# A hybrid decoder block on one core: one product for the bias rows, a prologue in order of arrival, and the next quarter's transposes moved among the last output tiles

## The reference

```
x   (2048, 1024)
h = rms_norm(x, g) ; z = h @ w_in        # 2304 columns: qa ka va | qr kr vr gr | up
A: 6 query heads, 2 key heads, window 128, blocks of 128, sinks,
   scores = q k^T / 8 + rel_bias[t5_bucket(dist)] , masked to 0 <= dist < 128
B: 6 retention heads in chunks of 128 with a carried 64x64 state, rotary, per-head norm, swish gate
C: trailing means over 2/4/8/16 positions, a 64x64 map per group
x = x + concat(A, B, C) @ w_out
x = x + relu(rms_norm(x) @ w_up)^2 @ w_down
return rms_norm(x, g_final)
```

## Time and profile before

| | |
|---|---|
| time, median of 3 runs (lowest to highest) | 2121.13 us (2120.67 to 2122.97) |
| the profiled execution: its own time, its span | 2121.23 us, 2119.4 us |
| PE busy | 2053.6 us (97%) |
| DVE, ACT, POOL busy | 1318.5, 918.5, 440.6 us |
| mixer: first product of quarters 0, 1, 2, 3 | 23.34, 232.48, 444.99, 653.40 us |
| end of the last output tile of the mixer | 858.57 us |

### The profile page before, as it was taken

One profiled execution on the slowest core, in us unless ns is written; L12 is line 12 of the kernel. 1 busy time (PEld: TensorE's weight loads), 2 busy tenths in 40 slices (PEclk: granted clock), 3 DMA queues, 4 the chain that ended last, 5 costly groups with the idle time before them and its releaser, 6 DMA issues.

```text
span 2119.4 us, 28140 instructions
## 1 busy us (share of the span) xinstructions
PE 2053.6 (97%) x10220; PEld 1728.1 (82%) x10220; DVE 1318.5 (62%) x1844; ACT 918.5 (43%) x1557; POOL 440.6 (21%) x363
## 2 busy tenths in 40 slices
PE   8998999999989998999999999999999999999998
PEld 6987798779877987788888888888788888888886
DVE  3346434643464447777777867777667757766666
ACT  4433443344334432654554654444433334433333
POOL 6256525652565355000000000000000000000001
PEclk9999999999999999999999999999999999999999
DMA  7132412241225122357776656677975667856562
GB/s 265 61 100 75 170 53 97 75 170 52 98 75 179 65 75 100 99 147 182 171 168 148 151 137 153 160 193 190 308 287 214 247 246 290 352 199 254 223 271 87
DMA packets 101956, 349.13 MB, mean 165 GB/s; under 512 B 10395, under 2 KB 12220, under 8 KB 84412
## 3 DMA queue, kind: packets, MB, share of 16 engines
q1 hardware_dynamic: 97212, 330.54, 48.5%
q10 hardware_dynamic: 4608, 16.78, 2.1%
HBM read 270.61 MB, written 76.68 MB: 164 GB/s over the span
## 4 chain that ended last, share of the span: by engine, by line
PE 85%; DVE 6%; issue 3%; POOL 3%; DMA 2%; ACT 1%; SPq 0%; ACTq 0%; DVEq 0%; POOLq 0%
PE bank L1977 27%; PE bank L1979 26%; PE bank L1978 26%; PE bank L2091 1%; PE bank L2120 1%; DMA d_raw<-in_wdn 1%; DVE pt L1449 1%; PE bank L2105 1%; PE bank L2208 1%; POOL r L809 1%; PE bank L2168 1%; DVE xq L1507 1%; DMA wraw<-in_wup 1%; POOL R L800 1%; DVE zt L1411 0%
## 5 line engine op out<-in xcount | busy, mean ns | idle before, releaser
L1977 PE MATMUL bank<-h_hi,w_lo 128*128 128x512 f32 x912 | 356.3, 391 | 1.8 <-ACT tA L1085 1.8
L1978 PE MATMUL bank<-h_lo,w_hi 128*128 128x512 f32 x912 | 355.1, 389 | 0.0
L1979 PE MATMUL bank<-h_hi,w_hi 128*128 128x512 f32 x912 | 355.1, 389 | 0.0
L1977 PE MATMUL bank<-d_hi,u_lo 128*128 128x512 f32 x896 | 349.0, 390 | 4.0 <-DVE d_lo L1849 4.0
L1979 PE MATMUL bank<-d_hi,u_hi 128*128 128x512 f32 x896 | 348.6, 389 | 0.0
L1978 PE MATMUL bank<-d_lo,u_hi 128*128 128x512 f32 x896 | 348.6, 389 | 0.0
L753 POOL TENSOR_TENSOR ring_lo<-stage,ring_hi 128x1024 fp32r<-128x1024 f32 x104 | 246.1, 2396 | 282.9 <-ACT ring_hi L905 282.8
L1226 ACT ACTIVATE u_hi<-u_raw 128x1024 fp32r<-128x1024 f32 x112 | 118.5, 1058 | 333.9 <-PE bank L1979 318.8
L883 POOL TENSOR_TENSOR var<-ssum,epsc 128x1 f32<-128x1 f32 x16 | 3.9, 241 | 1237.3 <-ACT sqj L1241 1237.3
L1849 DVE TENSOR_TENSOR u_lo<-u_raw,u_hi 128x1024 fp32r<-128x1024 f32 x112 | 137.0, 1223 | 179.6 <-ACT u_hi L1226 179.6
L1977 PE MATMUL bank<-ring_hi,hT_lo 128*128 128x384 f32 (+1 forms) x672 | 244.8, 364 | 0.2
(11 more groups left out here) (194 smaller groups left out, 3365.6 us busy)
## 6 DMA issues: line engine op xcount, KB each, us to landing
u_raw<-u_dram SPq DMA_DIRECT2D x56, 1024.0 KB, 4.8
d_raw<-in_wdn SPq DMA_DIRECT2D x56, 1024.0 KB, 6.9
stage<-in_wmix SPq DMA_DIRECT2D x108, 512.0 KB, 3.4
u_dram<-ur SPq DMA_DIRECT2D x32, 1280.0 KB, 9.4
wraw<-in_wup SPq DMA_DIRECT2D x128, 256.0 KB, 3.3
e_raw<-in_wdn SPq DMA_DIRECT2D x24, 1024.0 KB, 8.9
xn<-in_x SPq DMA_DIRECT2D x16, 512.0 KB, 4.8
xq<-in_x ACTq DMA_DIRECT2D x16, 512.0 KB, 6.0
```

Source lines behind the costliest of these rows:

```text
L1977: pe.matmul(dst, al, bh, start=(first and k == 0), stop=False, skip_group_check=chain)
L1978: pe.matmul(dst, ah, bl, start=False, stop=False, skip_group_check=chain)
L1979: last = pe.matmul(dst, ah, bh, start=False, stop=(final and k == n - 1), skip_group_check=chain)
```

## The change

What it does, by place:

- Bias: the 33x6 table is the stationary operand of one matmul whose result is 6 partitions x 384. DVE copies these 6 rows once. The store to DRAM reads each of the 6 rows 128 times.
- Prologue: SP issues the gain, the identity and `xn` 1 ahead of the bias tables; `mhalf` and `epsc` are set by POOL. ACT, DVE and PE take the blocks in order of arrival. The first two units are split by ACT and POOL before the loop.
- `norm_bank` uses (S0, S1) and (T1, OB) in turn. `norm_transposes`, `x_hi` and `x_lo` leave the head of a quarter; for the next quarter they stand among output tiles 12 to 15, in the last quarter not at all. `x_hi(b)` there waits for output tile 9 + 2b, since it writes over what the tile reads.
- `y_transposes` stand later: 0 behind tile 5, 1 behind `ret_outs(2)`, 2 behind tile 11, 3 behind tile 13. On DVE `yR_low` 0 and 1 stand later, `norm_ahead` earlier.
- Unit 28 (unit 1 of the next quarter) is split at the quarter's end; the loads of `xq` on ACT's queue move from the quarter's head to its first group tiles.

The diff, cut (counters renamed to `2 * NB * ahead + 2 * b + j`, and the last quarter's order on ACT, are left out):

```diff
         def norm_bank(b, j):
-            return ((T0, T1), (S0, S1), (dense[1], dense[2]), (OB, T0))[b][j]
+            return ((S0, S1), (T1, OB))[b % 2][j]
...
             sp.dma_start(xn[:, 0, :], x[0:P, :]).then_inc(x_full[0].sem, 16)
+            sp.dma_start(grow[:, :], gmix.to_broadcast([P, D])).then_inc(s_gain, 16)
+            sp.dma_start(ident[:, :], cview("ident")).then_inc(s_ident, 16)
+            sp.dma_start(xn[:, 1, :], x[P:2 * P, :]).then_inc(x_full[1].sem, 16)
             sp.dma_start(oneh, onehot).then_inc(s_rel, 16)
             sp.wait_ge(s_init, 1)
             sp.dma_start(relb[0:NBUCKET, :], rel_bias).then_inc(s_rel, 16)
-            sp.dma_start(mhalf[:, :], cview("mhalf")).then_inc(s_ident, 16)
-            sp.dma_start(epsc[:, :], cview("eps")).then_inc(s_ident, 16)
-            sp.dma_start(ident[:, :], cview("ident")).then_inc(s_ident, 16)
-            sp.dma_start(grow[:, :], gmix.to_broadcast([P, D])).then_inc(s_gain, 16)
-            for b in range(1, NB):
+            for b in range(2, NB):
...
-            sp.wait_ge(s_brow, NQH)
-            sp.dma_start(rows_dram.rearrange("h (p m) -> p h m", m=384), rrow).then_inc(s_rowst, 16)
+            sp.wait_ge(s_brow, 1)
+            sp.dma_start(rows_dram.rearrange("h (p m) -> h p m", m=384),
+                         rrow.rearrange("h (a m) -> h a m", a=1).to_broadcast([NQH, P, 384])).then_inc(s_rowst, 16)
...
     (POOL, end of a quarter)
-                for b in range(1, NB):
-                    inv_rms2(q, b)
+                inv_rms2(q, 1)
+                inv_rms2(q, 2)
+                if not last:
+                    split_lo(q, NU + 1)
+                inv_rms2(q, 3)
...
     (ACT)
             def mixer_act(q, last):
-                for b in range(NB):
-                    x_hi(q, b)
-                split_hi(q, 1)
                 split_hi(q, 2)
-                for b in range(NB):
-                    load_x(q, b)
...
                 square_x2(q, 0, last)
-                yR_high(q, 3)
-                if not last:
-                    square_x(q, NB + 3)
-                square_x2(q, 1, last)
...
+                else:
+                    square_x(q, NB + 3)
+                    square_x2(q, 1, last)
+                    x_hi(q, 0, True)
+                    yR_high(q, 3)
+                    x_hi(q, 1, True)
+                    x_hi(q, 2, True)
+                    square_x2(q, 2, last)
+                    x_hi(q, 3, True)
+                    split_hi(q, NU + 1)
+                    square_x2(q, 3, last)
...
     (DVE)
                 yP_low(q, 0)
-                yR_low(q, 0)
                 rot_a(q, 2)
                 rot_add(q, 2)
                 evac_x2(q, 5)
+                yR_low(q, 0)
...
                 decay_scores(q, 3)
+                evac_x2(q, 10)
+                norm_ahead(q, 0, last)
+                norm_ahead(q, 1, last)
+                evac_x2(q, 11)
                 yR_low(q, 2)
...
+                    x_lo(q, 0, True)
+                    evac_x2(q, 13)
+                    yR_low(q, 3)
+                    x_lo(q, 1, True)
                     norm_ahead(q, 3, last)
+                    x_lo(q, 2, True)
+                    evac_x2(q, 14)
+                    evac_x2(q, 15)
+                    x_lo(q, 3, True)
...
     (DVE, prologue)
-            for h in range(NQH):
-                if h == 4:
-                    x_norm(0, 0)
-                dve.wait_ge(s_browmm, h + 1)
-                dve.tensor_copy(rrow[:, h, :], bank[h][:, 0:384]).then_inc(s_brow, 1)
+            x_norm(0, 0)
+            x_norm(0, 1)
+            x_lo(0, 0, False)
+            x_norm(0, 2)
+            dve.wait_ge(s_browmm, 1)
+            dve.tensor_copy(rrow, bank[0][0:NQH, 0:384]).then_inc(s_brow, 1)
+            x_norm(0, 3)
...
     (PE)
                 pool_mix(q, 0)
+                out_tile(q, 5)
                 y_transposes(q, 0)
-                out_tile(q, 5)
...
                 ret_scores(q, 2)
-                y_transposes(q, 1)
                 out_tile_8_rest(q)
                 ret_outs(q, 2)
+                y_transposes(q, 1)
+                out_tile(q, 9)
                 qk_transposes(q, 3)
-                out_tile(q, 9)
+                out_tile(q, 10)
                 ret_scores(q, 3)
+                out_tile(q, 11)
                 y_transposes(q, 2)
-                out_tile(q, 10)
                 ret_outs(q, 3)
-                out_tile(q, 11)
                 out_tile(q, 12)
-                y_transposes(q, 3)
                 if closing:
                     h_transposes(0, 0)
+                else:
+                    norm_transposes(q, 0, True)
                 out_tile(q, 13)
+                y_transposes(q, 3)
                 if closing:
                     h_transposes(0, 1)
                     h_transposes(0, 2)
+                else:
+                    norm_transposes(q, 1, True)
+                    norm_transposes(q, 2, True)
                 out_tile(q, 14)
...
                 out_tile(q, 15)
+                if not closing:
+                    norm_transposes(q, 3, True)
...
     (PE, prologue)
+            norm_transposes(0, 0, False)
+            norm_transposes(0, 1, False)
+            pe.wait_ge(s_rel, 32)
+            pe.wait_ge(s_init, 1)
+            pe.matmul(bank[0][0:NQH, 0:384], relb, oneh, start=True, stop=True).then_inc(s_browmm, 1)
+            norm_transposes(0, 2, False)
+            norm_transposes(0, 3, False)
+            pe.wait_ge(s_brow, 1)
```

More of the change, by code:

```diff
@@ L745, in _ @@
             pool.wait_ge(s_pm, 6)
-            pool.wait_ge(s_ident, 48)
+            pool.wait_ge(s_half, 2)
             def split_lo(q, u):
@@ L831, in mixer_pool @@
             def mixer_pool(q, last):
-                for u in range(1, 6):
+                for u in range(2, 6):
                     split_lo(q, u)
@@ L938, in square_x2, with x_hi @@
                                accum_out=ssum2[:, bass.ds(q * NB + b, 1)]).then_inc(sq2_done.sem, 1)
-            def x_hi(q, b):
+            def x_hi(q, b, ahead):
+                if ahead:
+                    act.wait_ge(tile_done.sem, tile_done.now(q, T_OA + 9 + 2 * b))
                 for j in range(2):
[L942 to L945, removed]
+                    act.wait_ge(xtr_done.sem, xtr_done.now(q, 2 * NB * ahead + 2 * b + j))
                     act.activation(hT_hi[:, 4 * j:4 * j + 4, b * P:(b + 1) * P],
@@ L1156, in mixer_act @@
                             split_hi(q, 12 + 3 * (i // 2) + u)
+                    if i == 0:
+                        for b in range(NB):
+                            load_x(q, b)
                 yA_high(q, 3)
@@ L1198, in mixer_act @@
                     h_high(0, 1)
-                square_x2(q, 3, last)
-            for b in range(NB):
-                square_x(0, b)
+                    square_x2(q, 3, last)
+                else:
+                    square_x(q, NB + 3)
+                    square_x2(q, 1, last)
+                    x_hi(q, 0, True)
+                    yR_high(q, 3)
+                    x_hi(q, 1, True)
+                    x_hi(q, 2, True)
+                    square_x2(q, 2, last)
+                    x_hi(q, 3, True)
+                    split_hi(q, NU + 1)
+                    square_x2(q, 3, last)
+            square_x(0, 0)
+            square_x(0, 1)
+            x_hi(0, 0, False)
+            square_x(0, 2)
+            square_x(0, 3)
+            x_hi(0, 1, False)
             split_hi(0, 0)
+            x_hi(0, 2, False)
+            x_hi(0, 3, False)
+            split_hi(0, 1)
             with act.Fori(0, NQ - 1) as q:
@@ L1563, in mixer_dve @@
             def mixer_dve(q, last):
-                for b in range(NB):
-                    x_lo(q, b)
                 dve.wait_ge(o_done.sem, o_done.before(q, 3))
@@ L1965, in _ @@
                 pe.sem_inc(e.sem, e.primed)
-            pe.wait_ge(s_rel, 32)
-            pe.wait_ge(s_relw, 1)
-            for h in range(NQH):
-                pe.matmul(bank[h][:, 0:384], relw[:, h, :], oneh, start=True, stop=True).then_inc(s_browmm, 1)
-            pe.wait_ge(s_ident, 48)
-            pe.wait_ge(s_brow, NQH)
+            pe.wait_ge(s_ident, 16)
             def three(dst, pairs, first=True, final=True, chain=False):
```

82 lines of the change are left out of this document (34 added, 48 removed).

## The result

Four runs each: before 2121.78 us, after **2142.73 us** (2138.42 to 2146.93). The ratio is 1.0099, 95% interval 1.0087 to 1.0111. The forecast was 2108.0, range 2099.5 to 2115.5, so the sign was wrong as well.

What follows compares the result with a forecast made beforehand. PE was taken as the bound, with about 11 us open per mixer quarter, partly at low clock. Terms -6.1 - 5.45 - 1.8 + 1.1 - 1 = -13.25 on 2121.23 gave 2108.0 us, range 2099.5 to 2115.5.

Steps and rivals of the forecast that it cites:

- part 4: Prologue: first product at 19.5 to 20.7, tile 3 at 39 instead of 40.3; -1 us, between -4 and +2.
- rival (c): Prologue: slow bias store holds the weights, clock still low; quarter 0 gains nothing or loses 2; 2111 us, 17%.
- Part 1: First three quarters up to the end of tile 12: moving the y transposes is worth 0 in all.
- Rival (b): Mixer: low clock takes more behind the longer wait for the pool remainder; +9 us, 2117, chance 10%.
- Part 2: Changes of quarter, tile 12 to the next first product: gains of 6.1, 5.45 and 1.8 us.
- Part 3: Last quarter: tile 12 later and the second h_transposes waiting for yR_low(3); +1.1 us in sum.
- (a): Among the output tiles: the waits on y really go, 33.7 us gained in all; 2087.5 us, chance 3%.
- (d): Quarter's end: ACT's queue is held by a late load ahead of work tile 14 needs; 2126 us, 3%.
- (e): Waits added at the change of quarter (1.1 each) don't come, or the prologue keeps 3 to 4: 2103 us, 15%.

Runs made afterwards that it cites:

- e2: The changed kernel with the bias store reading six source partitions four apart (0, 4, 8, 12, 16, 20) instead of 0 to 5: 2113.99 us.
- e1: The changed kernel with the bias store reading 96 partitions, 8 copies each, instead of 6 with 128 copies each: 2113.94 us.
- e5: e1 with the moves of y transposes (blocks 0 to 2), block 3's qk transposes and yR_low 0 to 2 undone: 2101.42 us.
- e9: e1 with DVE's second pool remainder ahead of ret_y(1), and decay_scores(1) through yR_low(0) ahead of evac_x2(4) and (5): 2092.39 us.

## Why the prediction was wrong

**The step that failed: part 4, the bound of the store.** "From 6 partitions it may be as fast (3.5) or, were only 6 of the 16 DMA engines used, 9.4": the store took 34.3. The upper bound let each of the six engines go at the pace of the earlier trace rows, where all 128 partitions were read (and that row counts other loads too: 2.33 MB moved from 14.4 to 21.9 us, of which the store is 1.18). e2 shows that bound to be about right for six partitions that lie apart. It left out that neighbouring source partitions share a lower rate, 25 to 27 GB/s for a group, and no row of before reads so few. The value taken, "With 7.6 us, the row nearest", came from a row unlike it in the one thing that the change altered, the number of source partitions. The mechanism was right and stands as rival (c), with the threshold of 16 us from the row copy to SP's release. From the row copy, just before 16.09, to SP's release (50.41 + 2.72 = 53.1) it is 37 us, 21 over, and tile 3 came 23.0 us later than before. That e1 against after gives 28.8 is because tile 3 could have come 3 us sooner than before, and because PE then ran 5.3 us at half speed (63.31 to 68.6). Rival (c) ended at 2111 because it used the same bound of 9.4; e2, with the store back in 9.8 us, is as fast as e1, so at that price next to nothing was to be lost (0.65 us at tile 3).

**Part 4 otherwise.** First product at 19.71, forecast 19.5 to 20.7. The slow start at the first product took about 0.6 us, not 2: in e1 the products follow each other every 0.21 us from 19.88 to 21.32 and every 0.12 after. The prediction read such a pace as low clock. The profile's rows don't bear this out: they give the granted clock as 1.00 there, as they do in the earlier trace rows, so what makes PE slow in the prologue stays open. Tile 3 in e1 waited for nothing.

**Part 1, "0 in all".** The waits were walked rightly one by one: y(0) gave next to nothing, since PE then waits for the decayed scores before `ret_outs(1)`, 0.63 us in after and 0.98 in e1 (forecast 0.2 at most gained), the wait for y(1) went over to the pool remainder at 3.95 us (forecast 4.0), y(2)'s went. The `qk` transposes came 1.1 us later in e1, counted from `ret_outs(0)`, and 0.8 in after, not 0.6. What failed is the sum: waits were added as if each cost only its length. In e1 PE ran at the low level for 17 us more than in e5, 10 of them behind the `qk` wait of 2.0 and the remainder's 3.95 and 7 behind the wait for `hx`. Rival (b) named the clock, with 10% and 9 us; the size is near (8.5), the place only in part. Against e5 the moves cost 12.5 us, waits and clock together.

**Part 2.** Tile 12 to the first product: 16.5 us at the first change, forecast 15.5, before 19.8. y(3) waited 1.1 instead of 0.6, tile 14 not at all, and 0.86 us pass before the first product for which the trace names no releaser; that wait was not in the sum. It stands at both changes that are jumps back of the loop (0.86 and 0.63 us) and not at the third, which is none. In e1 the second of them, 0.95 us, is put down to DVE's last remainder for the next quarter. The clock stayed at full as forecast. At the third change 15.4 us, forecast 15.45.

**Part 3.** From the end of tile 12 to the first product of the second half e1 takes 22.4 us, before 21.5: +0.9, forecast +1.1. Over all, the last piece of the table is 4 us longer in after and e1 than in before; in e5 it is 0.1 longer. So e5 puts the rest of that down to part 1 as well, 3.4 us of it through the low spell behind `hx` whose cause is open.

**The other rivals.** (a) and (d) did not come; no load of `xn` held ACT.

**The whole.** With the store repaired and part 1 undone (e5) the rest of the change gives 20 us. The forecast for that rest was 13.3. The prologue gave 3.4 instead of 1, the changes of quarter 1 us less each, and the low clock shrank by 20.5 us, worth 10, where 3.6 had been counted: 13.3 + 2.4 - 2 + 6.6 is 20.3. That the sum fits is partly luck: the terms overlap, as part of the low clock lies within the changes of quarter, and no run parts them. So e1, only 6 us above the forecast, hides a part 1 that costs 12.5 and a rest that gives 7 more than forecast.

**Two sums of the range.** (e) with both its parts is 3 x 1.1 = 3.3 us of waits and 2 to 3 of prologue, so 2101.7 and not 2099.5, and half of (b)'s 9 us is 2112.5 and not 2115.5. The measured time lies far outside of either range.

## What to carry to other kernels

When an edit shrinks the number of partitions that a DMA reads, price the transfer by the bytes that each group of neighbouring partitions has to give, not by the rate of a wide transfer. Spread the source: in e1 that cost a broadcast copy of 0.2 us. Ask what the queue that waits for the landing has behind it. And when waits are moved, add the half-speed time behind each to its length: a wait that grows from 1 to 2 us may cost more than the wait.

## What the runs showed of the hardware that was not expected

Six source partitions side by side: 34.3 us for 1.18 MB, 50 and then 25 GB/s. Six that are four apart: 9.8 us, 151 GB/s. Ninety-six: 6.3 us. One at a time: 27 GB/s with the DMA engines 85% busy, 42.9 us. A busy DMA engine was thus no sign that bytes were moving fast.

The granted clock answers to small changes of order: 0.54 against 0.95 over the same 8 us, after waits of 3.95 and 3.29 us, with spells of 9 and of 3 us. Between before and e9 the low time falls from 37.5 to 3.4 us. Why a spell comes behind one wait and not behind another of like length (before has one of 3.2 to 3.3 us in each quarter, with 3 to 10 us of low clock behind it; e1 and e5 both have 3.18 us for `hx`, with 7 and with none) the runs leave open.
